# Twenty weight cells, eight fixed experts, and the second tile's split ahead of the routing

## The chip, the cores and the metric

One core of a Trainium2 chip runs the whole layer in one launch. The time is device microseconds (us) of that core. Engines: PE is TensorE (PEld its weight loads), DVE is VectorE, ACT is ScalarE, POOL is GpSimd, SP is SyncE, which here issues nearly all transfers between HBM and the on-chip memory. Matrix multiplies are in fp32, some of them with the operand split into two parts of type fp32r.

## The reference, cut to what matters

```python
def layer(x):                                     # x (256, 1024): 256 tokens, two tiles of 128
    x = x + hybrid_mixer(x, mem, ...)             # stick-breaking attention, RG-LRU, memory attention, w_out
    return x + moe_ffn(rms_norm(x, norm_ffn_g))   # the mixture of experts

def moe_ffn(t):                                   # 64 experts of 1024 x 256, and one shared
    scores = sigmoid(t @ w_router); choice = scores + router_bias
    # groups of 8 experts; the 4 groups with the largest sum of their top two stay
    _, eidx = top_k(where(emask, choice, -inf), 8)        # 8 experts for each token
    w = take(scores, eidx); w = w / (w.sum() + 1e-20) * 2.5
    routed = sum over experts e of gates[:, e] * ((silu(t @ wg[e]) * (t @ wu[e])) @ wd[e])
    return routed + (silu(t @ w_gate_sh) * (t @ w_up_sh)) @ w_down_sh
```

The inputs are drawn by `setup_inputs(seed=0)`. How many tokens pick an expert follows from them; the mean is 256 * 8 / 64 = 32.

## The kernel before

**Stages.** The mixer comes first (to about 128 us), then the router and the routing of the second half of the layer (to about 146 us), then 28 groups of experts, and the results are stored at the end. The residual stream after the mixer is the tile `x1` (128 partitions, 2 tiles of 128 tokens, 1024 columns; 8 KB a partition).

**Groups.** PE works on 128 rows ("slots") at a time. A group is a *single* (one expert with 128 slots), a *pair* (two experts with 64 each) or a *quad* (four with 32 each); the shared expert takes two groups, one for each tile of tokens. The first FIXED = 6 experts are *fixed*: they make three pairs whose place doesn't depend on the routing, so their weights can be loaded before it is known. The other 58 are ordered by their count of tokens (`key`, `rank`, `perm`): ranks 0 and 1 become singles, ranks 2 to HALF - 1 = 29 pairs, the ranks from HALF = 30 on quads. The list `kinds` gives the order of the groups. For each group PE gathers its tokens with 0/1 matrices `pick` (built by DVE, two groups, one "chunk", at a time), multiplies by gate and up (L1558), transposes (L1564, L1570), adds the group before back into the sums (`scatter`, L1588), and multiplies by down (L1580).

**Overflow.** The slots of an expert are a fixed capacity (`room_left`, `caps`): 128, 64 or 32 by its rank, 64 for a fixed one. What exceeds them is listed (`list_extra`) in blocks of 64 tokens, and `n_extra` is half the number of blocks, rounded up. After the 28 groups the results are stored (`store(0)`); then SP, ACT, DVE and PE each read `n_extra`, and where it is above zero they run the loop over `extra_pair`: SP loads gate, up and down of two experts (6 transfers of 1 MB into the cells 0 to 5, L463 and L466; where the list has but one block, the second expert is a filler and its weights are loaded all the same), PE gathers, multiplies and scatters as for a pair, ACT and DVE copy the sums again, and `store(1)` writes the whole output a second time.

**Cells.** Weights pass through CELLS = 18 cells of 8 KB a partition, each holding one part (gate, up or down) of one expert, 1 MB. `loads` lists all parts in the order of the groups; the first 18 have their own places in `cell_of`, each later one takes the cell that the groups free next (`wait_cell`: gate and up after the group's L1558 of that part, down after its L1580). The 18 first loads are the six fixed experts. Some of their cells are places that the mixer still uses, and SP waits for these: cells 12 and 13 lie in the place of `wo` (wait `wo_ps`), 14 on `x1_sq` (`ssq_act`), 15 on the router's tiles (`gates_dve`). SP issues in one fixed order.

**The routing.** ACT squares each tile of `x1`, takes a root, and writes `xhi` = the fp32r part of the normalised tile (`high_part`); DVE makes the rest, `xlo` (`low_part`). PE transposes `x1` and multiplies by the router (L1488), ACT applies the sigmoid (`score`), DVE picks the top eight (`route`, ending in `picked` L1091), PE sums the counts and positions (L1510 to L1520), DVE makes `posm` (L1115) and the first `pick` (L1130), and PE gathers the first chunk (L1527).

Of the kernel before, what the change touches and what calls it, by code (L numbers as in the profile page):

```python
# [5 lines left out]
def hybrid_decoder_layer(  # L6
# [26 lines left out]
    FIXED, HALF, TABLE = 6, 30, 8  # L33
# [4 lines left out]
    CELLS = 18  # L38
# [11 lines left out]
    kinds += ["pair"] * 2 + ["quad"]  # L50
# [26 lines left out]
    cell_of = dict(zip(loads, [16, 4, 17, 5, 3, 0, 1, 6, 2, 7, 8, 9, 10, 11, 12, 13, 14, 15]))  # L77
# [9 lines left out]
    KB = 1024  # L87
# [25 lines left out]
    cell_at = [o_ring + 8 * KB * i for i in range(12)] + [o_A + 16 * KB, o_A + 24 * KB, o_R + 8 * KB, o_O + 8 * KB, o_more, o_more + 8 * KB]  # L113
# [20 lines left out]
    wo = at("wo", o_A, [P, KD, D])  # L134
    xg = [at(f"xg{b}", o_A + 8 * KB * b, [P, KD, 2 * P]) for b in range(2)]
# [26 lines left out]
    pick = [at(f"pick{b}", o_V + 2 * KB * b, [P, NT, 2 * P], F32R) for b in range(2)]  # L162
# [25 lines left out]
    rt = Space(o_O + 12 * KB + 2080 + 6 * KB)  # L188
# [3 lines left out]
    rt = Space(o_O + 12 * KB + 2080 + 2 * KB)  # L192
# [6 lines left out]
    assert rt.offset <= o_O + 12 * KB + 2080 + 6 * KB  # L199
    rt = Space(o_O + 12 * KB + 2080 + 8 * KB)  # L200
# [49 lines left out]
    with ExitStack() as ctx:  # L250
# [300 lines left out]
        def _(act):  # L551
# [156 lines left out]
            for t in range(NT):  # L708
# [6 lines left out]
                if t == 0:  # L715
                    high_part(0)
# [5 lines left out]
            high_part(1)  # L722
# [1056 lines left out]
```

## Time and profile before

| | |
|---|---|
| median of 3 runs | 618.88 us (618.4 to 621.32) |
| profiled execution | 618.4 us, of which the span of the trace is 616.6 us |
| busy, share of the span | PE 93%, PEld 61%, DVE 32%, ACT 25%, POOL 3% |
| read from HBM | 225.90 MB |
| bytes moved, mean over the span | 369 GB/s |
| mean granted clock of TensorE | 0.982 of full |

The span runs from the first to the last instruction; the time of the execution is 1.8 us more. The page cuts the span into 40 slices of 15.4 us. PE's busy share is high nearly everywhere, but waits for transfers are partly hidden in it, since the matmuls' ends are modelled; the share of the 16 DMA engines and the GB/s tell in which slices the weights stream at full rate and in which they don't.

### The profile page before, as it was taken

How to read it: one execution, taken by the hardware profiler on the slowest of the kernel's cores; microseconds unless marked ns; L12 is line 12 of the kernel's file. 1: busy time of each engine (PE TensorE's matmuls, PEld its weight loads, DVE VectorE, ACT ScalarE, POOL GpSimd, SP SyncE). 2: the span in 40 equal slices, each digit the busy share in tenths (PEclk: the TensorE clock that was granted, in tenths of full speed). 3: DMA queues.
4: the chain of work that ended last, by engine and by line, in shares of the span. 5: the costliest groups of instructions: out<-in, count | busy, mean ns of one | idle time of the engine just before them, and what ended most of it. 6: DMA issues, size and time to landing. Idle time of an engine off the chain costs nothing.

```text
span 616.6 us, 10210 instructions
## 1 busy us (share of the span) xinstructions
PE 573.2 (93%) x4132; PEld 377.9 (61%) x4133; DVE 198.5 (32%) x527; ACT 151.1 (25%) x299; POOL 20.3 (3%) x78
## 2 busy tenths in 40 slices
PE   7999998997999999987999969999999999989774
PEld 6888774455665566654766636766676666656341
DVE  2247687756334222220222212122212222222102
ACT  4454246333211111110222111111111111111101
POOL 1003131000000000000000000000000000000000
PEclk9999999999999999996999999999999999999989
DMA  8995359533999999999999999999999999999993
GB/s 342 424 400 207 137 214 381 243 122 125 372 395 386 424 420 419 422 419 420 424 419 419 423 420 419 421 421 419 423 420 421 421 420 419 421 419 421 421 386 113
DMA packets 34000, 227.63 MB, mean 369 GB/s; under 512 B 3872, under 2 KB 4000, under 8 KB 8480
## 3 DMA queue, kind: packets, MB, share of 16 engines
q1 hardware_dynamic: 33808, 226.93, 89.7%
q8 instruction: 34, 0.56, 0.4%
q10 hardware_dynamic: 144, 0.03, 0.1%
q14 instruction: 14, 0.11, 0.0%
HBM read 225.90 MB, written 1.05 MB: 368 GB/s over the span
## 4 chain that ended last, share of the span: by engine, by line
PE 73%; DMA 16%; SPq 4%; DVE 3%; ACT 2%; issue 1%; DVEq 0%; ACTq 0%
PE ps L1558 25%; DMA cell_gu<-in_w_up_e 13%; PE ps L1580 12%; PE ps L1527 8%; PE ps L1326 7%; PE ps L1588 7%; PE ps L1448 4%; PE ps L1343 4%; DMA cell_d<-in_w_down_e 2%; SPq L442 2%; SPq L351 1%; PE ps L1333 1%; DMA wA<-in_w_qk 1%; PE ps L1564 1%; PE ps L1570 1%
## 5 line engine op out<-in xcount | busy, mean ns | idle before, releaser
L1558 PE MATMUL ps<-cell_gu,xg 128*64 128x256 f32 (+2 forms) x2112 | 208.8, 400 | 19.7 <-DMA cell_gu<-in_w_up_e 13.4
L1558 PEld LDWEIGHTS ps<-cell_gu,xg 128*64 128x64 f32 (+2 forms) x2112 | 135.3, 134 | 100.0 <-issue 47.0
L1580 PE MATMUL ps<-cell_d,e_hT 128*64 128x512 f32 (+2 forms) x528 | 102.2, 597 | 3.5 <-DMA cell_d<-in_w_down_e 2.6
L1272 DVE SCALAR_TENSOR_TENSOR ylo<-ps,gslot,yhi 128x512 fp32r<-128x512 f32 x56 | 42.1, 751 | 128.8 <-ACT yhi L749 128.8
L1213 DVE TENSOR_TENSOR e_h<-e_sg,ps 128x256 f32<-128x256 f32 x28 | 11.8, 421 | 180.8 <-ACT e_sg L737 180.8
L749 ACT ACTIVATE yhi<-ps,gslot 128x512 fp32r<-128x512 f32 x56 | 38.5, 688 | 127.1 <-PE ps L1580 127.1
L1580 PEld LDWEIGHTS ps<-cell_d,e_hT 128*64 128x64 f32 (+2 forms) x528 | 30.8, 128 | 59.4 <-issue 55.5
L737 ACT ACTIVATE e_sg<-ps 128x256 f32<-128x256 f32 x28 | 10.8, 385 | 209.5 <-PE ps L1558 209.5
L1527 PE MATMUL ps<-pick,xhi 128*128 128x256 f32 x224 | 48.3, 297 | 3.1 <-DVE pick L1130 3.1
L1588 PE MATMUL ps<-yhi,S 128*128 128x512 f32 x112 | 46.6, 416 | 0.6 <-DVE ylo L1272 0.6
L1527 PE MATMUL ps<-pick,xlo 128*128 128x256 f32 x224 | 45.0, 282 | 0.0
L1588 PE MATMUL ps<-ylo,S 128*128 128x512 f32 x112 | 44.0, 393 | 0.0
L1527 PEld LDWEIGHTS ps<-pick,xhi 128*128 128x128 f32 x224 | 34.7, 190 | 12.3 <-issue 11.8
L1527 PEld LDWEIGHTS ps<-pick,xlo 128*128 128x128 f32 x224 | 34.7, 191 | 0.0
L728 ACT ACTIVATE xg<-ps,vec 128x256 f32<-128x256 f32 x60 | 25.2, 471 | 26.5 <-PE ps L1527 26.4
L1326 PE MATMUL ps<-hT,wA 128*128 128x256 f32 x128 | 29.7, 395 | 1.3 <-DMA wA<-in_w_qk 1.3
L1448 PE MATMUL ps<-wo,yT 128*128 128x512 f32 x64 | 29.3, 601 | 0.0
L1326 PEld LDWEIGHTS ps<-hT,wA 128*128 128x128 f32 x128 | 25.4, 200 | 5.6 <-DMA wA<-in_w_qk 2.0
L1255 DVE TENSOR_TENSOR xg<-ps,vec 128x512 f32<-128x512 f32 x26 | 18.0, 692 | 32.7 <-PE ps L1527 32.7
L1588 PEld LDWEIGHTS ps<-yhi,S 128*128 128x128 f32 x112 | 21.1, 189 | 5.9 <-issue 1.2
L1588 PEld LDWEIGHTS ps<-ylo,S 128*128 128x128 f32 x112 | 21.1, 189 | 3.7
L1448 PEld LDWEIGHTS ps<-wo,yT 128*128 128x128 f32 x64 | 11.5, 190 | 12.6 <-issue 12.1
(308 smaller groups left out, 462.6 us busy)
## 6 DMA issues: line engine op xcount, KB each, us to landing
cell_gu<-in_w_gate_e SPq DMA_DIRECT2D x64, 1024.0 KB, 25.8
cell_gu<-in_w_up_e SPq DMA_DIRECT2D x64, 1024.0 KB, 26.3
cell_d<-in_w_down_e SPq DMA_DIRECT2D x60, 1024.0 KB, 26.1
wA<-in_w_qk SPq DMA_DIRECT2D x8, 512.0 KB, 10.5
wo<-in_w_out SPq DMA_DIRECT2D x1, 4096.0 KB, 13.2
cell_d<-in_w_down_e SPq DMA_DIRECT2D x8, 512.0 KB, 18.0
wR<-in_w_rest SPq DMA_DIRECT2D x3, 1024.0 KB, 28.0
wV<-in_w_v SPq DMA_DIRECT2D x1, 2048.0 KB, 17.6
```

Source lines behind the costliest of these rows:

```text
L442: sp.dma_start(cell_d[cell_of["down", e]][:, :, 512:D], ranked(w_down_e, chosen[e - first], KH)[:, :, 512:D]).then_inc(tail_loaded, 16)
L728: nc.scalar.mul(xg[c % 2][:, k, :], ps[:, Y[step % 2], k % 2 * 2 * P:(k % 2 + 1) * 2 * P], vec[:, GF + k:GF + k + 1]).then_inc(xg_act, 1)
L749: nc.scalar.mul(yhi[:, half * 512:(half + 1) * 512], ps[:, Y[half], :], gslot[:, g.index % 2:g.index % 2 + 1]).then_inc(yhi_act, 1)
L1255: nc.vector.tensor_tensor(xg[(g.chunk + 1) % 2][:, 2 * step:2 * step + 2, :], ps[:, Y[1], :].rearrange("p (k s) -> p k s", k=2), vec[:, c: ...
L1272: nc.vector.scalar_tensor_tensor(ylo[:, c], ps[:, Y[half], :], gslot[:, g.index % 2:g.index % 2 + 1], yhi[:, c].bitcast(F32), ALU.mult, AL ...
L1326: last = mm(b[:, 0:SEQ], w[:, k, c:c + P], hT[:, k, :], start=k == 0, stop=k == KD - 1)
L1343: last = mm(b, a[:, k, c:c + P], w[:, k, :], start=k == 0 and m == 0, stop=k == KD - 1 and m == 2)
L1448: last = mm(ps[:, ACC[2 * t + half], :], yT[:, k, t * P:(t + 1) * P], wo[:, k, half * 512:(half + 1) * 512], start=k == chunks[0], stop=k ...
L1527: last = mm(o, part[:, t, k, :], pick[c % 2][:, t, :], start=i == 0, stop=i == 3)
L1558: last = mm(ps[side * w:(side + 1) * w, U, cols], rows(k, slice(side * w, (side + 1) * w)), cell_gu[i][:, k, :], start=k == 0, stop=k == K ...
L1580: last = mm(ps[side * w:(side + 1) * w, Y[half], :], e_hT[:, kk, side * w:(side + 1) * w], cell_d[n][:, kk, half * 512:(half + 1) * 512], ...
L1588: last = mm(ps[:, ACC[2 * t + half], :], to_token[:, t * P:(t + 1) * P], y[:, half * 512:(half + 1) * 512], start=False, stop=sem is not N ...
```

## The change

- CELLS is 20. Cell 18 is the first 8 KB of the region `o_V` (the memory attention's `ca_p` and `ca_pT`, and formerly `pick`), cell 19 the place of `x1`. The two `pick` tiles move elsewhere: the second lies on `wg`, `upper`, `upper_off`, `ones_b` and `picked`, which are then no more needed. The results are no longer copied to `x1` but to `res`, on the first `xg`.
- FIXED is 8 and HALF is 28: four fixed pairs, then 56 ordered experts: two singles, the ranks 2 to 27 as 13 pairs, the ranks from 28 on as 7 quads. The group count stays 28; one routed pair near the end becomes the fixed pair at the start.
- SP issues the up part of the fifth fixed expert at `unit_ps` 33 (the memory attention's end) instead of after `wo_ps`, and the gate of the seventh when `x1` has been read (`split_dve`, `residual_ps`).
- ACT computes `high_part` of the second tile before the scores, and DVE `low_part` of it before `route` instead of behind it.
- PE gets `keep_clock`: three matmuls of 128x256 with no user before the wait for `picked`, and two behind the counts.

```diff
-    FIXED, HALF, TABLE = 6, 30, 8
+    FIXED, HALF, TABLE = 8, 28, 8
-    CELLS = 18
+    CELLS = 20
-    kinds += ["pair"] * 2 + ["quad"]
+    kinds += ["pair"] + ["quad"]
-    cell_of = dict(zip(loads, [16, 4, 17, 5, 3, 0, 1, 6, 2, 7, 8, 9, 10, 11, 12, 13, 14, 15]))
+    cell_of = dict(zip(loads, [16, 4, 17, 5, 3, 0, 1, 6, 2, 7, 8, 9, 10, 11, 18, 12, 13, 14, 19, 15]))
...
+    res = at("res", o_A, [P, NT, D])
-    pick = [at(f"pick{b}", o_V + 2 * KB * b, [P, NT, 2 * P], F32R) for b in range(2)]
+    pick = [pick0, at("pick1", r.offset, [P, NT, 2 * P], F32R)]
...
             load_fixed("gate", 6)
+            sp.wait_ge(unit_ps, 33)
+            load_fixed("up", 5)
             sp.wait_ge(wo_ps, len(projections))
-            load_fixed("up", 5)
             load_fixed("up", 6)
+            load_fixed("down", 5)
             sp.wait_ge(ssq_act, 6)
-            load_fixed("down", 5)
+            load_fixed("down", 6)
+            sp.wait_ge(split_dve, NT)
+            sp.wait_ge(residual_ps, 1)
+            load_fixed("gate", 7)
             sp.wait_ge(gates_dve, 1)
-            load_fixed("down", 6)
+            load_fixed("gate", 8)
...
-                if t == 0:
-                    high_part(0)
+                high_part(t)
...
-            high_part(1)
...
+            low_part(1)
             route()
             dve.wait_ge(route_dve, 1)
             link(nc.vector.tensor_scalar(repl[:], repl[:], HUGE, None, ALU.is_equal))
-            low_part(1)
...
+            def keep_clock(n):
+                for _ in range(n):
+                    mm(ps[:, Y[1], 0:SEQ], ident[:], xn2T[:, 0, :], start=True, stop=True)
+
+            keep_clock(3)
+
             pe.wait_ge(route_dve, 1)
...
             last.then_inc(count_ps, 1)
+            keep_clock(2)
```

SP, the last of the fixed loads and the first that take a freed cell. The number right behind `cell_gu` or `cell_d` is the cell. Before:

```order
L351 DMA cell_gu10_59<-in_w_gate_e 128x2048
L351 DMA cell_gu11_60<-in_w_gate_e 128x2048
L351 DMA cell_gu12_61<-in_w_up_e 128x2048 [waits wo_ps]
L351 DMA cell_gu13_62<-in_w_up_e 128x2048
L351 DMA cell_d14_81<-in_w_down_e 128x2048 [waits ssq_act]
L351 DMA cell_d15_82<-in_w_down_e 128x2048 [waits gates_dve]
```

After:

```order
L353 DMA cell_gu10_59<-in_w_gate_e 128x2048
L353 DMA cell_gu11_60<-in_w_gate_e 128x2048
L353 DMA cell_gu18_67<-in_w_up_e 128x2048 [waits unit_ps]
L353 DMA cell_gu12_61<-in_w_up_e 128x2048 [waits wo_ps]
L353 DMA cell_d13_82<-in_w_down_e 128x2048
L353 DMA cell_d14_83<-in_w_down_e 128x2048 [waits ssq_act]
L353 DMA cell_gu19_68<-in_w_gate_e 128x2048 [waits residual_ps,split_dve]
L353 DMA cell_gu15_64<-in_w_gate_e 128x2048 [waits gates_dve]
```

Two loads more stand ahead of the first one that needs a freed cell, one waits for an earlier event, and one stands between the waits for `ssq_act` and `gates_dve`.

DVE, from the pick of the eight experts to the first `pick`, before:

```order
L1091 TENSOR_SCALAR picked<-repl 128x128 [waits dve_chain]
L1111 TENSOR_SCALAR repl<-repl 128x128 [waits route_dve]
L1060 SCALAR_TENSOR_TENSOR xlo<-x_153,stat,xhi 128x1024 [waits split_act,dve_chain]
L1115 SCALAR_TENSOR_TENSOR posm<-ps,repl 128x128 [waits count_ps]
L1130 TENSOR_TENSOR pick_139<-iota_193,posm 128x256 [waits dve_chain]
```

After, the same place and what stands ahead of `route`:

```order
L1065 SCALAR_TENSOR_TENSOR xlo<-x_156,stat,xhi 128x1024 [waits split_act]
L1113 MEMSET grp 128x2x4 [waits consts,rb_loaded]
L1065 SCALAR_TENSOR_TENSOR xlo<-x_156,stat,xhi 128x1024 [waits split_act,dve_chain]
L1078 TENSOR_TENSOR choice<-score,rbias 128x128 [waits score_act]
...
L1096 TENSOR_SCALAR picked<-repl 128x128 [waits dve_chain]
L1117 TENSOR_SCALAR repl<-repl 128x128 [waits route_dve]
L1120 SCALAR_TENSOR_TENSOR posm<-ps,repl 128x128 [waits count_ps,dve_chain]
L1135 TENSOR_TENSOR pick_180<-iota_200,posm 128x256 [waits dve_chain]
```

The second `xlo` has moved from between `repl` and `posm` to ahead of `choice`.

PE, from the residual's matmuls to the first gather, after (before, the same without the rows of L1514):

```order
L1500 MATMUL ps<-x_156,ident 128x512 x4
L1514 MATMUL ps<-xn2T,ident 128x256 x3
L1521 MATMUL ps<-picked,upper 128x64 [waits order_pool,route_dve]
...
L1531 MATMUL ps<-ones_b,picked 64x1 x2
L1514 MATMUL ps<-xn2T,ident 128x256 x2
L1539 MATMUL ps<-pick_180,xhi 128x256 [waits pick_dve,split_dve]
```

The five added matmuls stand in the two places where PE waits for DVE.

## Rows read from the trace of the kernel before

**Rows 1.** The page's 40 slices of the span: DMA busy tenths and GB/s.

```profile
DMA  8995359533999999999999999999999999999993
GB/s 342 424 400 207 137 214 381 243 122 125 372 395 386 424 420 419 422 419 420 424 419 419 423 420 419 421 421 419 423 420 421 421 420 419 421 419 421 421 386 113
```

**Rows 2.** Stages (start:end us, length, busy of five engines, clock, DMA share, GB/s).

```profile
145.00:150.00 5.00, 4.35 (x33) 3.96 (x34) 3.08 (x15) 2.52 (x6) 0.00 (x0) 1.00 0.00 0
...
160.00:200.00 40.00, 38.35 (x300) 23.51 (x302) 16.44 (x58) 8.19 (x17) 0.00 (x0) 1.00 0.97 385
200.00:603.00 403.00, 380.40 (x3058) 244.09 (x3054) 87.49 (x220) 71.18 (x144) 0.00 (x0) 0.97 1.01 418
```

**Rows 3.** SP's timeline, issues of weight loads (start, us, engine, line, tile, count).

```profile
96.77 0.99 SPq L351 DMA_DIRECT2D cell_gu<-in_w_gate_e  x2
132.68 0.80 SPq L351 DMA_DIRECT2D cell_gu<-in_w_up_e  x2
...
154.12 5.02 SPq L351 DMA_DIRECT2D cell_gu<-in_w_gate_e  x4
...
197.52 4.42 SPq L351 DMA_DIRECT2D cell_gu<-in_w_up_e  x4
```

**Rows 4.** Timeline of all engines through the routing, 134 to 145 us.

```profile
135.06 1.28 ACT L721 ACT_TABLE_LOAD   x1
...
138.30 0.31 ACT L721 ACTIVATE score<-ps,stat 128x64 f32<-128x64 f32 x1 [1.63 <-PE ps L1488]
138.51 1.14 ACT L706 ACTIVATE xhi<-x,stat 128x1024 fp32r<-128x1024 f32 x1
...
142.98 0.20 PE L1510 MATMUL ps<-picked,upper 128*128 128x64 bf16 x1 [1.23 <-DVE picked L1091]
...
143.22 1.28 DVE L1060 SCALAR_TENSOR_TENSOR xlo<-x,stat,xhi 128x1024 fp32r<-128x1024 f32 x1
...
143.43 0.20 PE L1520 MATMUL ps<-ones_b,picked 128*64 128x1 bf16 x2
...
144.43 0.28 DVE L1115 SCALAR_TENSOR_TENSOR posm<-ps,repl 128x128 f32<-128x128 f32 x1
```

**Rows 5.** Pieces of the chain that ended last (start, us, what): single matmul groups.

```profile
85.38 3.46 PE ps L1326 x16
...
150.32 3.60 PE ps L1558 x32
...
161.74 3.58 PE ps L1580 x16
...
207.18 1.96 PE ps L1588 x8
```

**Rows 6.** Timeline of the last group and the end, 584 to 617 us.

```profile
584.48 5.16 PE L1558 MATMUL ps<-cell_gu,xg 128*32 128x256 f32 x64 [3.58 <-DMA cell_gu<-in_w_gate_e]
...
599.80 0.38 ACT L737 ACTIVATE e_sg<-ps 128x256 f32<-128x256 f32 x1 [18.16 <-PE ps L1558]
...
601.80 1.93 PE L1580 MATMUL ps<-cell_d,e_hT 128*32 128x512 f32 x16 [0.61 <-DVE e_hT L1216]
...
606.33 1.92 PE L1580 MATMUL ps<-cell_d,e_hT 128*32 128x512 f32 x16 [2.60 <-DMA cell_d<-in_w_down_e]
...
609.94 0.47 PE L1588 MATMUL ps<-yhi,S 128*128 128x512 f32 x1 [0.57 <-DVE ylo L1272]
...
611.15 0.69 DVE L1281 COPY x<-ps 128x512 f32<-128x512 f32 x1 [0.76 <-PE ps L1588]
```

**Rows 7.** SP's instructions that read `n_extra`, by line (ns min/median/max, start us).

```profile
L454 SPq TENSOR_LOAD <-n_extra x1: 280/280/280, 615.6 to 615.6; - x1
L454 SPq FUSED_REGOPS  x1: 158/158/158, 615.9 to 615.9; - x1
L455 SPq COMPARE_BRANCH  x1: 53/53/53, 616.2 to 616.2; - x1
```

**Rows 8.** DMA issues from 150 to 153.5 us: one load alone, us to landing.

```profile
cell_d<-in_w_down_e SPq DMA_DIRECT2D x1, 1024.0 KB, 4.9
```

More of the change, by code:

```diff
@@ L109, in __call__ @@
             return t
-    cell_at = [o_ring + 8 * KB * i for i in range(12)] + [o_A + 16 * KB, o_A + 24 * KB, o_R + 8 * KB, o_O + 8 * KB, o_more, o_more + 8 * KB]
+    cell_at = [o_ring + 8 * KB * i for i in range(12)] + [o_A + 16 * KB, o_A + 24 * KB, o_R + 8 * KB, o_O + 8 * KB, o_more, o_more + 8 * KB, o_V, o_O]
     cell_gu = [at(f"cell_gu{i}", cell_at[i], [P, KD, DE]) for i in range(CELLS)]
@@ L187, in hybrid_decoder_layer @@
     choice = rt("choice", [P, NT, NE])
-    rt = Space(o_O + 12 * KB + 2080 + 6 * KB)
+    rt = Space(o_O + 14 * KB + 6 * KB)
     cand = rt("cand", [P, NT, NE])
@@ L191, in hybrid_decoder_layer @@
     gatew = rt("gatew", [P, NT, NE])
-    rt = Space(o_O + 12 * KB + 2080 + 2 * KB)
+    rt = Space(o_O + 14 * KB + 2 * KB)
     pos_T = rt("pos_T", [NE, SEQ])
@@ L198, in hybrid_decoder_layer @@
     ids = rt("ids", [1, NV], I32)
-    assert rt.offset <= o_O + 12 * KB + 2080 + 6 * KB
-    rt = Space(o_O + 12 * KB + 2080 + 8 * KB)
+    assert rt.offset <= o_O + 14 * KB + 6 * KB
+    rt = Space(o_O + 14 * KB + 8 * KB)
     e_h = rt("e_h", [P, KH, P])
@@ L205, in hybrid_decoder_layer @@
     gates2 = rt("gates2", [P, NT, NE, 2], F32R)
+    pick0 = rt("pick0", [P, NT, 2 * P], F32R)
+    assert rt.offset <= r.offset
     ident = r("ident", [P, P])
     ones = r("ones", [P, P])
+    pick = [pick0, at("pick1", r.offset, [P, NT, 2 * P], F32R)]
+    wg = r("wg", [P, 2, 2, HD])
     upper = r("upper", [P, P], BF16)
+    upper_off = r("upper_off", [P, P], BF16)
     ones_b = r("ones_b", [P, P], BF16)
-    brow = at("brow", r.offset, [P, NE])
-    upper_off = at("upper_off", r.offset + 4 * NE, [P, P], BF16)
-    r.offset += 8 * NE
+    picked = r("picked", [P, NT, NE], BF16)
+    brow = r("brow", [P, NE])
     vec = r("vec", [P, 50])
@@ L448, in store @@
                         sp.wait_ge(sem, 2 * n + half + 1)
-                        sp.dma_start(out[0, t * P:(t + 1) * P, c], x1[:, t, c]).then_inc(stored, 16)
+                        sp.dma_start(out[0, t * P:(t + 1) * P, c], res[:, t, c]).then_inc(stored, 16)
                 sp.wait_ge(stored, 64 * (n + 1))
@@ L769, in result @@
                 c = slice(half * 512, (half + 1) * 512)
-                nc.scalar.copy(x1[:, 0, c], ps[:, ACC[half], :]).then_inc(out_act, 1)
+                nc.scalar.copy(res[:, 0, c], ps[:, ACC[half], :]).then_inc(out_act, 1)
             for g in groups:
@@ L1280, in result @@
                 c = slice(half * 512, (half + 1) * 512)
-                nc.vector.tensor_copy(x1[:, 1, c], ps[:, ACC[2 + half], :]).then_inc(out_dve, 1)
+                nc.vector.tensor_copy(res[:, 1, c], ps[:, ACC[2 + half], :]).then_inc(out_dve, 1)
             for g in groups:
```

2 lines of the change are left out of this document (removed).

## The prediction

> **What bounds the kernel now.** I read the slices of the span first. In them [rows 1] the reader sees two parts: to about slice 10 the transfers come and go (137, 122, 125 GB/s in some slices), and from slice 11 on the weights stream at 386 to 424 GB/s without a hole almost to the end. The table of stages says the same: 418 GB/s and a DMA share of 1.01 over 403 us [rows 2]. So behind the routing the time is bytes: one part of an expert is 1.049 MB, 2.5 us at 418 to 420 GB/s. Next SP's timeline: the two gates issued at 96.8 us are the last until 132.7, and the next after the fixed ones is the first load that needs a freed cell, at 154.1 us, when PE has finished the first gates [rows 3]. From 145 to 150 us not a byte moves [rows 2]: the cells are full and none is free. What is loaded before 154 us costs nothing; what is not costs 2.5 us each. The end is set by the last weights: PE waits for them at 606.3, and from there to the end of the span it is 10.2 us of dependent work [rows 6].
>
> **Cells and order of the loads.** Two cells more mean two more parts loaded in the dead time. The up part of the fifth expert now goes out at about 117 us, when the queue is empty, and the gate of the seventh at about 142 us, into the hole from 142 to 151 (the only load there, that on `gates_dve`, leaves at 151 as before). Neither meets other traffic. Gain: 2 x 2.5 = **-5.0 us**, as the stream behind 154 us is bound by bytes. But from 160 to 200 us it moves only 385 GB/s [rows 2], as PE frees the cells of pairs one after the other and the queue catches up with it (at 197.5 SP issues two loads the moment they are freed [rows 3]). With four pairs before the first quad this stretch lasts a group longer. At the 385 GB/s of this stretch, 15 us more of it lose 15 x (1 - 385/418) = 1.2 us at the worst, and nothing if the queue is two loads behind by then, which the 4.9 - 2.5 = 2.4 us from issue to first data suggests [rows 8]. I take **+0.3** (0 to 1.2). Later on, 20 cells can only make the holes rarer, and there are none in 403 us. The fixed pair in front replaces a routed one at the end: same bytes, same matmuls, so 0.
>
> **Routing.** DVE's second `xlo`, 1.28 us, stands between `repl` and `posm` [rows 4]. The counts for which `posm` waits are ready at 143.63, `posm` starts at 144.43, so 0.8 us are to be had, not 1.28. Ahead of the scores ACT now does `xhi` (1.14 us) before the sigmoid's table load: root ready at 135.6, xhi to about 136.9, table 1.28 to 138.2, the first score 0.31 to 138.5, the second to 138.85; it ended at 138.61 before [rows 4]. So +0.25. DVE's low part (136.9 + 0.1 + 1.28 = about 138.8) ends beside the second score. Net **-0.5** (-0.8 to +0.3). `keep_clock`: a 128x256 matmul is 3.46 / 8 = 0.43 us [rows 5], three are 1.3 us where PE sits idle 1.23 us before the counts [rows 4], which begin 0.25 later now; two are 0.86 us, from 143.9 to 144.7, before `pick` is ready at about 145. Cover holds on both, cost 0 (0.1 at most); the granted clock is 1.00 around there [rows 2], so nothing is won either.
>
> Up to here: -5.0 + 0.3 - 0.5 = **-5.2 us**, or 618.4 - 5.2 = 613.2.
>
> **HALF = 28 and what it does to the tokens.** This has no row; it is decided by the inputs. I evaluated the reference's routing for its own draw (seed 0) and counted tokens per expert. The eight fixed ones have 16, 18, 21, 21, 13, 20, 31 and 29. Of the others the largest are 77, 74, 56 and 53, and **29 experts have more than 32** tokens, the 28th and the 29th 34 each. Before, ranks 30 and up stand in quads with 32 slots; rank 30 has 31 tokens, so nothing overflows, `n_extra` is 0, and SP ends a fraction of a us after its branch at 616.2 [rows 7]. After, the 29th, rank 28, is the first in a quad: 34 tokens in 32 slots. One block, so `n_extra` is 1, and all four engines run `extra_pair` once, for two tokens. The two experts that left the ordered list (31 and 29 tokens) were not above 32, so they took nothing off the top. It is not a close call: the scores would have to move two tokens of the same expert (noise of 1e-4 on the scores never changed the 34).
>
> The price, step by step, in the times of the trace before. The reads and the branch: SP reads `n_extra` at 615.6, 0.28 + 0.16 + 0.02 us, then a branch of 0.05 [rows 7], and then the numbers of two experts in the same way: 615.6 + 3 x 0.46 + 0.2 = 617.2 for the first issue. The loads: one alone lands after 4.9 us [rows 8], each further one 2.5 us later: gates (2) at 624.6, ups (4) at 629.6, downs (6) at 634.6. The multiplies: a gate or up of a pair is 3.60 [rows 5], but after a wait the clock is lower: the last quad's gate took 5.16 after 3.58 us idle [rows 6]. Gate 624.6 + 5.2 = 629.8, up 3.6 to 633.4. From the end of up to the first down it is 2.0 us (599.8 to 601.8 [rows 6]): 635.4, and the downs have landed. Down 3.58 [rows 5] to 639.0; from its end to the scatter 1.7 us (608.25 to 609.94 [rows 6]): 640.7. The scatter of both halves 1.96 [rows 5]: 642.7. From there to the end, through copy, store and its receipt, 5.4 us (611.15 to 616.6 [rows 6]): 648.1. That is 648.1 - 616.6 = **+31.5 us**. All of it is exposed: it begins when the store has landed, and nothing is left to hide it. Gathering, 32 matmuls, is done under the loads. Bounds: 28 if the clock stays up, the loads start 1 us sooner and the gaps shrink by a us; 38 if gate, up, down and scatter all run at half the clock (5 us more) and jumping to the loop costs a us or more on SP. The branch taken is an operation that no row shows.
>
> On that last point the Trainium skill has a rule that speaks against the change (Runtime: NRT & Kernel Launch, Instruction fetch mechanics): a taken branch whose target lies outside the pages just fetched must wait for a fetch from memory before it goes on. It gives no price. The branch of the trace is not taken, so no row bears it out; by it the sum would end above the middle of my bounds.
>
> **Sum:** 618.4 - 5.2 + 31.5 = 644.7; I say **645 us**. The profiled execution stands 0.5 us under the median of the three runs, so the same sum on the median is 645.2.
>
> **Rivals.**
> 1. *No extra pair* (0.10): `n_extra` stays 0, because the chip's draw or the kernel's own order of counts differs from my count. Then the time is 613.2 (612 to 615), faster than before by 0.9%. It decides at one point: whether the 29th count is above 32. For it: only that I have no row of the counts. Against it: the trace before shows no extra pair with HALF = 30, as my count demands.
> 2. *The extra pair costs more than summed* (0.06): cold code on four engines and a cold clock throughout, above 38 us: 653 to 660.
> 3. *The head start is lost too* (0.04): the queue is starved through the fourth pair, or a wait put before `gates_dve` holds the last fixed load up, and the 5 us come to 0: 618.4 + 0.3 + 31.5 = 650. Against it: the stream has 403 us without a hole.
> 4. The forecast (0.80).
>
> **Numbers.** A measurement tells 0.5% (3.1 us) from no change. Faster by more: rival 1, 0.09; within: 0.01; slower: 0.90. The range: from 618.4 - 6 + 28 = 640 to 618.4 - 4 + 38 = 652, widened by 1 us on each side for the gap between runs, 639 to 653; it holds the forecast and rival 3, 0.84, and leaves rival 1 out.
>
> **What would show it.** In the profile after, the read from HBM tells at once: 225.90 + 6 x 1.05 = 232.2 MB with the extra pair, 225.9 without. Loads of L470 and L473 and eight stores, not four, at the end. SP's load of `gate` 7 near 142 us and DMA idle again to 151. `posm` about 0.5 us earlier. The last weights of the 28th group landing near 601 instead of 606.3, and the first store's end near 610. I am wrong on the head start if that landing isn't 4 to 6 us earlier, and on the whole if no L470 runs.

## The result, and the profile after

The changed kernel takes 643.08 us, the median of 6 runs (641.36 to 645.64), beside 621.03 us for the kernel before in 6 runs of the same comparison (618.4 to 622.67). The ratio is 1.0365, 95% interval 1.0332 to 1.0398: slower by 3.65%. The prediction was 645 us, range 639 to 653. The profiled execution is the one of 641.36 us, with a span of 639.6 us; that of the kernel before is 618.4 us with a span of 616.6 us.

The page of the kernel after, for rows 1: the DMA tenths and GB/s of its 40 slices (now 16.0 us each), and the total of the transfers.

```profile
DMA  8985549466999999999999999999999999999583
GB/s 345 424 357 198 235 170 425 176 246 236 388 398 397 390 422 420 423 420 420 421 421 421 420 420 420 422 421 421 421 421 420 422 420 422 417 424 405 189 325 135
...
HBM read 232.19 MB, written 2.10 MB: 366 GB/s over the span
```

The stream that was whole to the end [rows 1] now breaks off (189 GB/s), comes back (325) and ends (135). The read from HBM has grown by 6.29 MB, six parts of 1.05 MB, and 2.10 MB are written instead of 1.05: both are the mark of the extra pair.

Its stages, with the columns of rows 2: the hole of the routing, the stretch of the fixed pairs, and the long one behind it.

```profile
145.00:150.00 5.00, 5.00 (x41) 3.98 (x41) 2.23 (x11) 3.36 (x8) 0.00 (x0) 1.00 0.01 3
160.00:200.00 40.00, 39.05 (x286) 24.23 (x286) 14.81 (x51) 7.64 (x15) 0.00 (x0) 1.00 0.97 389
200.00:215.00 15.00, 15.00 (x154) 9.12 (x152) 3.87 (x9) 2.98 (x6) 0.00 (x0) 1.00 0.98 394
200.00:600.00 400.00, 376.94 (x3070) 241.39 (x3068) 88.23 (x221) 71.86 (x145) 0.00 (x0) 0.98 1.00 415
```

The stretch of fixed pairs moves 389 GB/s (385 before), and the slower rate goes on for 15 us more, as assumed: from 200 to 215 us it is 394 GB/s here and was 424 in the kernel before. SP's timeline of the same kernel, for rows 3:

```profile
115.88 16.08 SPq L353 DMA_DIRECT2D cell_gu<-in_w_up_e  x2
132.01 1.92 SPq L353 DMA_DIRECT2D cell_d<-in_w_down_e  x2
140.80 8.71 SPq L353 DMA_DIRECT2D cell_gu<-in_w_gate_e  x2
152.19 0.81 SPq L353 DMA_DIRECT2D cell_gu<-in_w_up_e  x2
```

An up part goes out at 115.9, a gate at 140.8, the last fixed load behind `gates_dve` at about 149. The first load that takes a freed cell goes out at 152.19, where it was 154.12. The routing, for rows 4, in ACT's, DVE's and PE's rows:

```profile
134.62 1.15 ACT L713 ACTIVATE xhi<-x,stat 128x1024 fp32r<-128x1024 f32 x1 [0.61 <-DVE stat L1052]
135.78 1.28 ACT L727 ACT_TABLE_LOAD   x1
...
137.08 0.52 ACT L727 ACTIVATE score<-ps,stat 128x64 f32<-128x64 f32 x2
...
140.55 1.46 PE L1514 MATMUL ps<-xn2T,ident 128*128 128x256 f32 x6
141.61 0.23 DVE L1096 TENSOR_SCALAR picked<-repl 128x128 bf16<-128x128 f32 x1
...
142.46 1.13 PE L1514 MATMUL ps<-xn2T,ident 128*128 128x256 f32 x4
142.64 0.29 DVE L1120 SCALAR_TENSOR_TENSOR posm<-ps,repl 128x128 f32<-128x128 f32 x1 [0.54 <-PE ps L1531]
```

`posm` starts 1.03 us behind `picked`, instead of 1.73 (142.70 to 144.43), and now it waits for the counts, not for `xlo`.

And the end, for rows 6 and 7: the last downs of the 28th group, DVE's last copy of the sums ahead of the first store, SP's read of `n_extra`, and the extra pair on all engines (L470 and L473 are SP's loads, L1611 the gather, L1570 gate and up, L1592 down, L1600 the scatter).

```profile
599.65 1.92 PE L1592 MATMUL ps<-cell_d,e_hT 128*32 128x512 f32 x16 [1.32 <-DMA cell_d<-in_w_down_e]
...
604.47 0.69 DVE L1286 COPY res<-ps 128x512 f32<-128x512 f32 x1 [0.75 <-PE ps L1600]
...
L461 SPq TENSOR_LOAD <-n_extra x1: 278/278/278, 607.4 to 607.4; - x1
...
607.82 0.37 DVE L1229 TENSOR_TENSOR pick<-iota,posm 128x64 fp32r x2 [2.66 <-issue]
609.54 0.36 DVE L1229 TENSOR_TENSOR pick<-iota,posm 128x64 fp32r x2 [1.36 <-issue]
609.70 0.88 SPq L470 DMA_DIRECT2D cell_gu<-in_w_gate_e  x2
609.96 0.69 PE L1611 MATMUL ps<-pick,xhi 128*128 128x128 f32 x2 [5.53 <-DVE pick L1229]
...
611.86 0.93 SPq L473 DMA_DIRECT2D cell_d<-in_w_down_e  x2
...
618.07 8.24 PE L1570 MATMUL ps<-cell_gu,ov_xg 128*64 128x256 f32 x64
...
628.45 3.65 PE L1592 MATMUL ps<-cell_d,e_hT 128*64 128x512 f32 x16 [0.76 <-DMA cell_d<-in_w_down_e]
...
633.71 0.47 PE L1600 MATMUL ps<-yhi,S 128*128 128x512 f32 x1 [1.61 <-ACT yhi L769]
...
635.06 1.90 SPq L456 DMA_DIRECT2D out<-res  x4
```

The last weights are there 6.7 us earlier (606.33 to 599.65), SP reads `n_extra` 8.2 us earlier, and then 32.2 us follow to the end of the span at 639.6. Without the pair the span ends about 1.0 us behind that read (616.6 - 615.6 before, 610.1 - 609.1 in e1 below), so counted from the read the pair costs 31.2 us, and 31.2 - 8.2 = +23.0 us, which is 639.6 - 616.6.

The read is an uneven mark, though. It starts 2.87 to 2.93 us behind the start of DVE's last copy in the four programs that run the pair (after, e2, e8, e9), and 4.2 to 5.2 us behind it in the ten that don't (4.45 in before). Those 1.5 us belong to the difference between a program with the pair and one without. Counted from the last copy, 35.1 us follow in after and 5.4 in before and in e1: the pair costs 29.7 us net, the copy itself comes 6.7 us earlier (611.15 to 604.47), and 29.7 - 6.7 is again +23.0.

### The profile page after: what moved, and what is told of

Read it like the earlier page. It is cut to its first block, busy times and chain, and to the rows that moved or that the text cites. A ratio compares the mean times of both kernels' runs of the same rounds, so it can differ in the third digit from the quotient of the medians.

```text
span 639.6 us, 10584 instructions
## 1 busy us (share of the span) xinstructions
PE 593.9 (93%) x4270; PEld 393.1 (61%) x4271; DVE 203.7 (32%) x536; ACT 155.6 (24%) x309; POOL 20.3 (3%) x78
## 3 DMA queue, kind: packets, MB, share of 16 engines
HBM read 232.19 MB, written 2.10 MB: 366 GB/s over the span
## 4 chain that ended last, share of the span: by engine, by line
PE 71%; DMA 19%; SPq 4%; ACT 3%; DVE 2%; issue 1%; DVEq 0%; ACTq 0%
PE ps L1570 24%; DMA cell_gu<-in_w_up_e 13%; PE ps L1592 13%; PE ps L1539 7%; PE ps L1600 7%; PE ps L1331 5%; DMA cell_d<-in_w_down_e 4%; PE ps L1453 4%; PE ps L1348 3%; SPq L449 2%; DMA x_in<-in_x 1%; SPq L353 1%; PE ps L1338 1%; PE ps L1576 1%; PE ps L1582 1%
## 5 line engine op out<-in xcount | busy, mean ns | idle before, releaser
L1570 PE MATMUL ps<-cell_gu,xg 128*64 128x256 f32 (+2 forms) x2112 | 206.9, 395 | 18.5 <-DMA cell_gu<-in_w_up_e 13.8
L1570 PEld LDWEIGHTS ps<-cell_gu,xg 128*64 128x64 f32 (+2 forms) x2112 | 134.6, 133 | 97.7 <-issue 44.1
L1592 PE MATMUL ps<-cell_d,e_hT 128*64 128x512 f32 (+2 forms) x544 | 105.8, 597 | 3.2 <-DMA cell_d<-in_w_down_e 2.1
L1592 PEld LDWEIGHTS ps<-cell_d,e_hT 128*64 128x64 f32 (+2 forms) x544 | 32.1, 128 | 60.9 <-issue 58.3
L1600 PE MATMUL ps<-yhi,S 128*128 128x512 f32 x116 | 48.1, 415 | 2.2 <-ACT yhi L769 1.6
L1600 PE MATMUL ps<-ylo,S 128*128 128x512 f32 x116 | 45.5, 392 | 0.0
L1331 PE MATMUL ps<-hT,wA 128*128 128x256 f32 x128 | 28.1, 380 | 1.4 <-DMA wA<-in_w_qk 1.4
L1260 DVE TENSOR_TENSOR xg<-ps,vec 128x512 f32<-128x512 f32 x26 | 18.0, 692 | 32.2 <-PE ps L1539 32.2
L1600 PEld LDWEIGHTS ps<-yhi,S 128*128 128x128 f32 x116 | 21.9, 189 | 8.4 <-ACT yhi L769 2.5
L1600 PEld LDWEIGHTS ps<-ylo,S 128*128 128x128 f32 x116 | 21.9, 189 | 3.7
## 6 DMA issues: line engine op xcount, KB each, us to landing
cell_d<-in_w_down_e SPq DMA_DIRECT2D x62, 1024.0 KB, 26.3
cell_d<-in_w_down_e SPq DMA_DIRECT2D x8, 512.0 KB, 17.8
wV<-in_w_v SPq DMA_DIRECT2D x1, 2048.0 KB, 17.8
```

The costliest lines, as they stand in the source:

```text
L1260: nc.vector.tensor_tensor(xg[(g.chunk + 1) % 2][:, 2 * step:2 * step + 2, :], ps[:, Y[1], :].rearrange("p (k s) -> p k s", k=2), vec[:, c: ...
L1331: last = mm(b[:, 0:SEQ], w[:, k, c:c + P], hT[:, k, :], start=k == 0, stop=k == KD - 1)
L1570: last = mm(ps[side * w:(side + 1) * w, U, cols], rows(k, slice(side * w, (side + 1) * w)), cell_gu[i][:, k, :], start=k == 0, stop=k == K ...
L1592: last = mm(ps[side * w:(side + 1) * w, Y[half], :], e_hT[:, kk, side * w:(side + 1) * w], cell_d[n][:, kk, half * 512:(half + 1) * 512], ...
L1600: last = mm(ps[:, ACC[2 * t + half], :], to_token[:, t * P:(t + 1) * P], y[:, half * 512:(half + 1) * 512], start=False, stop=sem is not N ...
```

## The experiments

The theory (A) was that of the prediction: cells and routing win about 5 us, the extra pair loses about 31 us. The rivals (B) differ from run to run and stand in the expectations. "After" is the changed kernel.

**e1: the changed kernel with `n_extra` forced to 0.**

```diff
-    link(nc.vector.tensor_scalar(end[:, 0:1], end[:, NE - 1:NE], 0.5, 0.25, ALU.mult, ALU.add))
+    link(nc.vector.tensor_scalar(end[:, 0:1], end[:, NE - 1:NE], 0.0, 0.25, ALU.mult, ALU.add))
```

> The changed kernel with n_extra forced to 0, so the loop over the extra pair is skipped (the two tokens that overflow their quad lose that one expert's contribution). Theory A (the extra pair is the whole loss, about 31 us, all exposed; cells and routing gain): 643.1 - 31 = 612 us, 0.986 to 0.991 of the kernel before, span of the profile about 608. Theory B (part of the loss is elsewhere: the new order of groups, colliding loads or the new waits on SP): above 618 us, a ratio of 0.995 or more.

Measured 612.96 us (611.83 to 616.77, 6 runs), before 619.06, ratio 0.991 [0.9884, 0.9937]. All the rest of the change is faster than before by 0.9%, and the pair accounts for the whole loss: 643.08 - 612.96 = 30.1 us between the medians. These stem from two comparisons, in which the kernel before took 621.03 and 619.06 us; each against its own, it is 22.05 + 6.10 = 28.2 us.

**e2: the kernel before with `n_extra` forced to 1.** The list is empty, so both sides of the pair are fillers; nothing is added to the result.

```diff
-    link(nc.vector.tensor_scalar(end[:, 0:1], end[:, NE - 1:NE], 0.5, 0.25, ALU.mult, ALU.add))
+    link(nc.vector.tensor_scalar(end[:, 0:1], end[:, NE - 1:NE], 0.0, 1.0, ALU.mult, ALU.add))
```

> The kernel before with n_extra forced to 1: the list of overflows is empty, so both experts of the pair are fillers, the output is unchanged, and only the loop over the pair and the second store are added. Theory A: the price of the pair belongs to the pair and not to the new layout: 621.0 + 31 = 652 us (650 to 654), ratio 1.050, and the stretch from the read of n_extra to the end 32 us. Theory B (the pair is dear only in the changed kernel, by the moved pick and result tiles): under 645 us.

Measured 649.88 us (649.23 to 650.65, 4 runs), ratio 1.0494 [1.0466, 1.0523], which is +30.8 us on 619.06. The pair costs about the same in a kernel that has none of the other parts. In its timeline the first load and the multiplies stand as they do in after, 8.1 us later; ahead of them the last copy and the read of `n_extra`, and below the same two rows of e1:

```profile
612.57 0.69 DVE L1281 COPY x<-ps 128x512 f32<-128x512 f32 x1 [0.75 <-PE ps L1588]
L454 SPq TENSOR_LOAD <-n_extra x1: 278/278/278, 615.5 to 615.5; - x1
617.81 0.88 SPq L463 DMA_DIRECT2D cell_gu<-in_w_gate_e  x2
...
626.18 8.34 PE L1558 MATMUL ps<-cell_gu,ov_xg 128*64 128x256 f32 x64
```

```profile
604.68 0.69 DVE L1286 COPY res<-ps 128x512 f32<-128x512 f32 x1 [0.75 <-PE ps L1600]
L461 SPq TENSOR_LOAD <-n_extra x1: 274/274/274, 609.1 to 609.1; - x1
```

From the copy to the read it is 2.9 us in e2 and 4.4 in e1. e2 differs from before (4.45) in two constants of one DVE instruction only, so the shorter time goes with the pair and not with the new layout; why, no run shows. From the last copy to the end of the span it is 35.2 us in e2 and 5.45 in before: 29.8 us for the pair, as in after.

**e3: as e1, but with 18 cells.** Eight fixed experts, the loads of fixed parts in the order of before, and the last six of the 24 fixed parts only when cells come free.

```diff
-    CELLS = 20
+    CELLS = 18
...
-            sp.wait_ge(unit_ps, 33)
-            load_fixed("up", 5)
             sp.wait_ge(wo_ps, len(projections))
+            load_fixed("up", 5)
             load_fixed("up", 6)
-            load_fixed("down", 5)
             sp.wait_ge(ssq_act, 6)
-            load_fixed("down", 6)
-            sp.wait_ge(split_dve, NT)
-            sp.wait_ge(residual_ps, 1)
-            load_fixed("gate", 7)
+            load_fixed("down", 5)
             sp.wait_ge(gates_dve, 1)
-            load_fixed("gate", 8)
+            load_fixed("down", 6)
```

> As e1 (no extra pair; the two overflowing tokens lose one expert's contribution), but with 18 cells: cells 18 and 19 are gone, the parts of the fourth fixed pair wait for freed cells. Theory A (the two cells are worth 2 x 2.5 us): 613.0 + 4.7 = 617.7 us, ratio 0.996 to 0.999. Theory B (the gain of e1 comes from the routing's order or from the fixed pair in front, not from the cells): 613 to 614.5 us, ratio below 0.993.

Measured 617.95 us (12 runs), before 619.47, ratio 0.9978 [0.9954, 1.0002]. Against e1 that is 617.95 - 612.96 = 5.0 us for two cells, and 4.6 with each against its own kernel before; the intervals of the two ratios leave room for some 2 us either way. That fits 2 x 2.5. Its SP timeline has no load between 97 and 133 us, and its last downs start at 607.04, against 599.87 in e1:

```profile
607.04 1.92 PE L1587 MATMUL ps<-cell_d,e_hT 128*32 128x512 f32 x16 [2.75 <-DMA cell_d<-in_w_down_e]
```

These are 7.2 us, of which 1.5 were there before any of the edit (SP loads the router at 91.22 in e3's profiled execution, at 89.73 in e1's); 5.7 are left.

**e4: as e1, with ACT's and DVE's order of before in the routing.**

```diff
-                high_part(t)
+                if t == 0:
+                    high_part(0)
...
+            high_part(1)
...
-            low_part(1)
             route()
             link(nc.vector.tensor_scalar(repl[:], repl[:], HUGE, None, ALU.is_equal))
+            low_part(1)
```

> As e1, but the second tile's high part is again behind the scores and its low part between repl and posm. Theory A: +0.7 us on e1, 613.7 us; in the profile posm starts 0.7 us later after picked (1.7 us instead of 1.0). Theory B (the move does nothing, as something else is late by then): 613.0 and the first gather as early after picked as in e1.

Measured 613.85 us (612.54 to 614.73, 6 runs), ratio 0.9903 [0.9882, 0.9925]: 0.9 us above e1 (0.5 with each against its own kernel before), less than these intervals can tell apart. The traces are clearer. In e4, and then in e1:

```profile
141.60 0.23 DVE L1098 TENSOR_SCALAR picked<-repl 128x128 bf16<-128x128 f32 x1
...
143.33 0.28 DVE L1122 SCALAR_TENSOR_TENSOR posm<-ps,repl 128x128 f32<-128x128 f32 x1
```

```profile
141.63 0.23 DVE L1096 TENSOR_SCALAR picked<-repl 128x128 bf16<-128x128 f32 x1
...
142.66 0.29 DVE L1120 SCALAR_TENSOR_TENSOR posm<-ps,repl 128x128 f32<-128x128 f32 x1 [0.54 <-PE ps L1531]
```

`picked` comes at the same time: moving `xhi` and `xlo` ahead of the scores costs nothing here, and `posm` comes 0.67 us sooner. The first freed cell is reloaded at 152.22 in e1, at 152.87 in e4.

**e5: as e1, without the five matmuls that have no user.**

```diff
-            keep_clock(3)
...
-            keep_clock(2)
```

> As e1, without the five matmuls that have no user. Theory A: no difference, 613.0 us within 0.5, granted clock 1.00 from 140 to 150 us as before. Theory B (they keep TensorE's clock up during the gather): the clock falls to half in the gather and the first chunk takes up to 4 us more, 615 to 617 us.

Measured 615.09 us (612.4 to 617.36, 6 runs), ratio 0.9914 [0.9884, 0.9944], 2.1 us above e1. The stretch from 143 to 150 us, in e5 and then in e1 (columns as in rows 2, the clock third from the end):

```profile
143.00:150.00 7.00, 6.24 (x29) 5.86 (x30) 2.90 (x14) 2.42 (x6) 0.00 (x0) 0.51 0.24 102
```

```profile
143.00:150.00 7.00, 6.72 (x51) 5.33 (x51) 4.15 (x18) 3.36 (x8) 0.00 (x0) 1.00 0.27 112
```

Without the five the granted clock is 0.51 through the gather, that is 1.2 GHz; with them it is 1.00 (2.4 GHz). The first gates start at 150.78 instead of 148.50 and the first freed cell is reloaded at 154.50 instead of 152.22. Here B held in the profiled executions: the matmuls are worth 2.3 us in the trace, not 0. The medians alone don't show it: the ratios of e5 and e1, each to its own kernel before, are 0.9914 and 0.9910. Against e4, from the same comparison as e5, e5 is 1.2 us longer, although e4's `posm` comes 0.7 us later.

**e10: the kernel before with the same five matmuls.**

```diff
+            keep_clock(3)
             pe.wait_ge(route_dve, 1)
...
             last.then_inc(count_ps, 1)
+            keep_clock(2)
```

> The kernel before with the five userless matmuls of the change around the counts, and nothing else. Theory A (without them the clock falls in some executions of the kernel before between 143 and 154 us, which costs about 2 us then): the slow half of its runs goes, median 618.4 to 619.0, 0.5 to 1 us under the kernel before, highest under 620. Theory B (the fall in e5 comes of the shorter wait for the picks in the new order only): no difference in median or spread.

Measured 619.02 us (618.06 to 620.16, 12 runs), before 619.23 (617.18 to 625.23, 17 runs), ratio 0.9993 [0.9972, 1.0014]. No difference in the median, as B said; the spread, where B expected none either, did differ (the highest of 12 is 620.16, two of the 17 of before are above 622), and these runs don't say why. In the profiled execution of before, the clock from 143 to 150 us is 1.00 without the matmuls; e2, which has the same order there and none of them either, shows 0.81, and its first gates start 60.7 us behind the load of the router (90.94 to 151.65), where before and e10 take 59.5 (90.73 to 150.25, 89.47 to 148.98). So A's premise holds for e2: without the five, the clock can fall in this order too, and it costs 1.2 us then. Why the order of before could keep its clock through 2.0 us of idle time ahead of the gather, while e5's didn't through 1.34 us, isn't settled by these runs.

**e6: 20 cells with six fixed experts, HALF = 30.** The last two cells take the gates of the first two routed experts, which SP loads as soon as the routing is known.

```diff
-    FIXED, HALF, TABLE = 8, 28, 8
+    FIXED, HALF, TABLE = 6, 30, 8
-    kinds += ["pair"] + ["quad"]
+    kinds += ["pair"] * 2 + ["quad"]
...
-            load_fixed("gate", 7)
-            sp.wait_ge(gates_dve, 1)
-            load_fixed("gate", 8)
-            for part, e in loads[CELLS:]:
+            for part, e in loads[3 * FIXED:]:
...
-                wait_cell(sp, part, e)
+                if (part, e) in taken_from:
+                    wait_cell(sp, part, e)
+                elif cell_of[part, e] == 15:
+                    sp.wait_ge(gates_dve, 1)
```

> Twenty cells, the routing's new order, but six fixed experts and HALF = 30 as before: the two added cells take the gates of the first two routed experts as soon as their numbers are known (about 149 us), so nothing overflows. Theory A (cumulated loads are cells plus freed cells once the queue has caught up with PE near 200 us, so two cells are worth 5 us whoever's weights fill them): 621.0 - 5 to -7 = 614 to 616 us, ratio 0.989 to 0.992. Theory B (the gain comes only from loads issued in the dead time before 149 us, for which eight fixed experts are needed): 618 to 621 us, ratio 0.995 to 1.0. The profile: DMA idle from 141 to 149 either way; landing of the last weights near 600 (A) or 605 (B) against 606.3.

Measured 613.25 us (612.3 to 614.71, 6 runs), ratio 0.9905 [0.9883, 0.9927], and the same kernel again as **e12**:

> The kernel of e6 again, on the same chip as e11 and the kernel before, as the other side of that comparison. Theory A and B: 613.3 us within 1, ratio 0.990; clock 1.00 from 143 to 150 us.

612.77 us (611.06 to 613.93, 5 runs), ratio 0.9884 [0.9856, 0.9912]. This version has slots for all tokens and runs no extra pair, and it is faster than both kernels, than the kernel before by 1.0 and 1.2%. In e6, SP's first routed gates, and the stretch from 160 to 200 us:

```profile
150.54 2.74 SPq L353 DMA_DIRECT2D cell_gu<-in_w_gate_e  x4
...
160.00:200.00 40.00, 38.92 (x324) 23.64 (x326) 15.04 (x54) 7.68 (x15) 0.00 (x0) 1.00 1.01 414
```

The two cells are filled 10 us later than a fixed gate could fill the first of them (140.8), but the stretch then moves 414 GB/s instead of 383 in e1. Both streams come out alike (last downs at 600.23, against 599.87). So the fourth fixed pair isn't needed for the gain of the cells.

**e11: e6 without the five matmuls** (the diff of e5).

> As e6 (20 cells, six fixed experts, HALF = 30), without the five userless matmuls. Theory A (the clock falls during the first gather and the first gates, 143 to 150 us, and the stream's start is late by 2 us): 615 to 616 us, granted clock near 0.5 there in the profile. Theory B (e5's median was an accident of few runs): as e12 within 0.5 us.

Measured 615.19 us (611.45 to 618.34, 8 runs), before 620.0, ratio 0.9916 [0.9886, 0.9946]: 2.4 us above e12. The clock from 143 to 150 us, in e11 and in e12:

```profile
143.00:150.00 7.00, 5.30 (x32) 5.20 (x33) 3.47 (x15) 1.68 (x4) 0.00 (x0) 0.61 0.00 0
```

```profile
143.00:150.00 7.00, 6.72 (x52) 5.28 (x52) 3.90 (x18) 3.36 (x8) 0.00 (x0) 1.00 0.01 2
```

From the first gather matmul to the first gates it takes 6.97 us in e11 (145.34 to 152.31) and 4.61 in e12 (143.63 to 148.24): 2.36 us, near the difference of the medians, 2.42 in one comparison, though the intervals of the two ratios overlap. The second pair of kernels, in another order of groups, so repeats what e5's trace shows.

**e7: as the changed kernel, but HALF = 32 and 29 groups.** Room for all tokens without an extra pair, by one group more.

```diff
-    FIXED, HALF, TABLE = 8, 28, 8
+    FIXED, HALF, TABLE = 8, 32, 8
-    kinds += ["pair"] + ["quad"]
+    kinds += ["pair"] * 3
```

> The changed kernel with HALF = 32: three pairs more at the end and one quad less, 29 groups instead of 28, the last group a pair; nothing overflows. Theory A (the stream of bytes sets the time, PE has some 20 us of waits to spare for a group of 15 us): 621.0 - 6 to -9 = 612 to 615 us, ratio 0.986 to 0.991. Theory B (the 29th group, about 15 us of PE, comes onto the path since PE already is 93% busy): 621 to 628 us, ratio 1.0 or more.

Measured 617.82 us (616.7 to 618.91, 12 runs), ratio 0.9973 [0.9959, 0.9986], between the two theories. The last stretches of its span:

```profile
590.00:600.00 10.00, 10.00 (x65) 5.67 (x66) 1.50 (x2) 1.37 (x2) 0.00 (x0) 1.00 0.82 321
600.00:612.00 12.00, 9.60 (x56) 4.67 (x52) 3.40 (x8) 3.19 (x6) 0.00 (x0) 1.00 0.08 31
```

The weights have landed before 600 us (what moves behind that is mostly the store), but PE is busy for all of the ten microseconds before that, and its last down starts at 605.25. The same weights in one group more have made PE the bound at the end: from 566.8 to 603.3 us the chain of waits is PE alone, and behind it come hand-offs between ACT, DVE and PE, with no load of weights. That eats 617.82 - 612.96 = 4.9 us (one comparison), nearly all that the cells won.

**e8: the extra pair without the filler's three loads.** The second side of the pair multiplies by the first expert's cells, and its rows add nothing.

```diff
-    for i0, e in ((0, e0), (3, e1)):
+    for i0, e in ((0, e0),):
...
-    down((2, 5), ov_y_ps)
+    down((2, 2), ov_y_ps)
```

> The changed kernel with its extra pair, but the filler expert's three weight loads are left out; its side of the pair multiplies the first expert's weights for no token, so the output is the same. Theory A (the pair is bound by TensorE: 8 us of gather and 8.2 us of gate and up, from a wait on, at half its clock; the transfers only by 0.8 us): 643.1 - 0.5 to -1.5 = 642 us, ratio 1.035. Theory B (bound by its 6 MB, as my prediction had it): 643.1 - 7.5 = 635.6 us, ratio 1.024.

Measured 644.08 us (642.87 to 645.52, 6 runs), ratio 1.0387 [1.0362, 1.0412]. With half of the bytes the pair isn't cheaper (after: 1.0365 [1.0332, 1.0398]). In its timeline nothing waits for a transfer, and gate and up take longer than in after:

```profile
620.57 9.44 PE L1570 MATMUL ps<-cell_gu,ov_xg 128*64 128x256 f32 x64
```

**e9: e8 with 14 userless matmuls of 128x256 ahead of the pair's gather,** while PE waits for the store, for `n_extra` and for the `pick` tiles.

```diff
+                for _ in range(14):
+                    mm(ps[:, Y[1], 0:SEQ], ident[:], iota1[:, 0:SEQ], start=True, stop=True)
                 pe.wait_ge(ov_pick_dve, 4 * i + 4)
```

> As e8 (extra pair without the filler's loads), with 14 matmuls of 128x256 that have no user put ahead of the pair's gather, while TensorE waits for the picks. Theory A (the pair is bound by TensorE at half its clock): gather 8 to 4.5 us, gate and up 9.4 to 7.1 us, in all 644.1 - 5 to -6 = 638 to 639 us. Theory B (it is bound by the serial hand-offs and the store, not by TensorE's clock): within 1 us of 644.1.

Measured 638.48 us (637.27 to 640.49, 4 runs), ratio 1.033 [1.0308, 1.0352]: 5.6 us less than e8, or 5.4 with each against its own kernel before. PE's rows (the trace has two records for each of the 14, as for those of `keep_clock`):

```profile
604.57 6.28 PE L1609 MATMUL ps<-iota,ident 128*128 128x256 f32 x28
...
615.25 7.13 PE L1570 MATMUL ps<-cell_gu,ov_xg 128*64 128x256 f32 x64 [0.29 <-DVE ov_xg L1233]
```

From the gather's first matmul to the first gate it is 8.10 us in e8 (612.47 to 620.57) and 4.75 in e9 (610.50 to 615.25), and gate and up take 7.13 instead of 9.44: 3.35 + 2.31 = 5.7 us. With three loads, then, 5.6 of the pair's some 30 us are PE's low clock.

With all six loads, as in after, the chain that ends last runs through the last down part:

```profile
612.35 16.01 DMA cell_d<-in_w_down_e
```

That part lands at 628.36 and the downs start 0.09 us behind it, so a warm PE alone would not have started them sooner. e8 and e9 show what the clock is worth only where the filler's loads are gone.

## Why the prediction was right, and where its steps were not

**The tokens.** The step that decided the sign, the overflow of a quad's 32 slots, held: 232.19 MB were read (232.2 predicted), L470 and L473 ran, and the stores were doubled. (That the expert has just 34 tokens stands in no trace; the traces show that there was something to do, and one pass of it.) Rival 1 (no extra pair, 613.2 us) was the right price for the other case, as e1 shows (612.96), but not this case.

**The cells: -5.0.** Right, and separately measured: e3 against e1 gives 5.0 (4.6 to 5.7 by the ways of counting above). The loads went where the prediction put them (115.9 for 117, 140.8 for 142), and the stretch of low rate was a group longer, as said: from 200 to 215 us it moved 394 GB/s where before moved 424. By the prediction's own formula that is 15 x (1 - 394/424) = 1.1 us, near its upper bound of 1.2 and not 0.3; no run tells it apart at the end. A slip of reading on the way: slice 11 of [rows 1] moves 372 GB/s, and not 386 or more.

**The routing: -0.5.** The mechanism was right, the size a little small. I had put +0.25 on the first score for the moved `xhi`. But `picked` comes at the same time with both orders (141.60 in e4, 141.63 in e1), since both scores then run in one row of 0.52 us behind a table load that ends at 137.06; the second is ready at 137.60 in after and at 137.52 in e4. Only the 0.7 us of `posm` are left: 1.73 - 1.03 = 0.70, of the 0.8 to be had.

**`keep_clock`: 0.** Wrong. I read the granted clock of 1.00 from before [rows 2] and concluded that "nothing is won". It is the clock of another order of work. With the order of after and no such matmuls the clock does fall, to 0.51 in e5 and 0.61 in e11, and the first gates are 2.3 and 2.4 us late for it in the traces; even in the order of before it fell in e2 (0.81). It should have been bounded: the gather stands on PE between the routing and the first gates, 4.61 us long at full clock (e12), and whatever part of it runs at half clock delays every freed cell behind it. In the sum it didn't show, because the profiled execution of before has 1.00 there too and both sides of the subtraction had a warm PE. That the term came out right for before against after is in part luck; it was wrong as a statement of what the matmuls do.

**Up to here: -5.2.** The last weights came 6.7 us earlier in the one profiled execution (606.33 to 599.65), more than the 4 to 6 that the prediction had named as the sign of the head start. 1.0 of it is not the change's: SP's load of the router, ahead of all that the change touches, stood at 90.73 and stands at 89.69:

```profile
90.73 0.33 SPq L404 DMA_DIRECT2D w_rt<-in_w_router  x1
```

```profile
89.69 0.33 SPq L406 DMA_DIRECT2D w_rt<-in_w_router  x1
```

It varies from run to run (90.94 in e2, 89.47 in e10, both with the order of before). What is left is 5.7 us. Of medians, e1 against before says 619.06 - 612.96 = -6.1. The 8.2 us by which `n_extra` was read earlier hold 1.5 more, which go with the pair (e2).

**The extra pair: +31.5.** 31.2 by the trace of after, counted from the read as in the prediction, or 29.7 counted from the last copy; 30.8 by e2's median, and 30.1 or 28.2 by e1's. That 31.5 came so near is in part luck: the steps inside were off and made up for each other, and the picture was wrong in one point. "Gathering, 32 matmuls, is done under the loads": not wholly. PE comes out of its wait at half clock and the gather with what belongs to it takes 8.1 us (609.96 to 618.07), so by the time PE asks for gates and ups they are there: no wait for them is in the trace. The second gate lands at 617.0 (6.8 us behind its issue at 610.23), so 1.0 us of the gather sticks out. The windows of after, for the clock:

```profile
607.00:610.00 3.00, 0.04 (x1) 0.04 (x1) 0.73 (x4) 0.00 (x0) 0.00 (x0) 0.50 0.00 0
610.00:612.00 2.00, 2.00 (x10) 2.00 (x10) 0.00 (x0) 0.00 (x0) 0.00 (x0) 0.50 0.56 147
...
618.00:620.00 2.00, 2.00 (x11) 1.23 (x13) 0.31 (x2) 0.37 (x1) 0.00 (x0) 0.50 1.06 446
620.00:622.00 2.00, 2.00 (x20) 1.25 (x18) 0.00 (x0) 0.00 (x0) 0.00 (x0) 0.91 0.96 406
```

| step, from the read of `n_extra` | predicted | after |
|---|---|---|
| first load issued | 1.6 | 2.3 |
| gate and up done | 17.8 | 18.9 |
| first down starts | 19.8 | 21.0 |
| scatter starts | 25.1 | 26.3 |
| end of the span | 32.5 | 32.2 |

Up to the scatter the chain was 1.2 us longer than summed, 0.7 of them from the taken branch and the loop's entry; the scatter, the copies, the store and its receipt were 1.5 us shorter. The wait for the downs, which I took to have landed, is 0.76 us: loads and PE end almost together, the loads a little later, so that taking away one side alone wins next to nothing. e8 takes away half of the loads and nothing is won, because PE's side stands (in the profiled execution gate and up even take 9.44 us instead of 8.24 at a clock that rises later). e9 raises the clock on top of that and 5.6 us go. Warming PE with all six loads in place wasn't run; by the trace of after the last part's landing at 628.36 leaves it little to win.

The upper bound of 38 was summed too low. In the gather a row of two records follows the last after 0.43 us at clock 0.50 (after) and after 0.22 at 1.00 (e9), 1.9 times. On the 12.7 us of gate, up, down and scatter at full clock this is, as an estimate, some 10 us above the sum and not 5. It wasn't put to the test, as the clock rose at about 620 us.

The taken branch: behind the sentence on the Trainium skill's rule (Runtime: NRT & Kernel Launch, Instruction fetch mechanics) the trace now has two numbers. SP's first load in the loop goes out 2.3 us after its read (1.6 summed), and DVE shows gaps of 2.66 and 1.36 us "issue", in which it waits for nothing that the profile shows. The rows don't say how much of them is fetching.

**Rivals 2 and 3.** Both fell. The pair cost less than 38 us by every count above, and the head start was kept (e1, and e3 for its size).

## What to carry to other kernels

Where a capacity is cut to make room for something else, count the inputs against it first: two tokens over the limit cost about 30 us where the rest of the change had won 6, and two more cells without the cut won as much (e6). The serial tail behind the last store had no cover, and PE came into it at half clock (0.50), so such matmuls should be priced at that clock and not as hidden; but the loads of the tail form a second chain of nearly the same length, and both have to become shorter before the time does. The clock seen in one order of work doesn't tell what another order will have: userless matmuls in a wait that exists anyway cost nothing measurable here (e10: 0.9993) and kept 2.3 and 2.4 us in two traces.

## What the runs showed of the hardware

- PE's granted clock after a gap: after 5.5 us of idle it was 0.50 in after from 607 to 620 us, although PE was busy without a hole from 610 on, and in e8 it was 0.50 still from 620 to 622. With the userless matmuls in the gap (6.28 us in e9) it stayed at 1.00.
- With an idle gap of only 1.34 us before the gather, and one of 1.18 ahead of the counts (e5, e11), the clock was 0.51 and 0.61 from 143 to 150 us; with 0.28 us (e1, e12) it was 1.00. The order of before has gaps of 2.0 and 1.2 us there, and a clock of 1.00 in the kernel before and of 0.81 in e2. What decides it is open.
- Six transfers of 1 MB issued into an empty queue within 3.1 us (609.70 to 612.79) had all landed by 628.36, 18.7 us after the first issue; the estimate from rows 8 and the 2.5 us for each further one was 17.4.
- From one DVE instruction to the next in the loop's entry 2.66 and 1.36 us passed without a wait, both in after and in e2 (2.67 and 1.36): the entry costs the same in both programs.
- From DVE's last copy to SP's read of `n_extra` behind the store, 2.87 to 2.93 us passed in the four programs that then run the pair, 4.2 to 5.2 in the ten that don't. In the trace the slowest of the stores lands 2.6 us after its issue in after and e2 and 3.7 us after it in before and e1. The cause is open.
